# A streaming encoder step on one core: identity first, zero matmuls in a wait, constants moved up, and the last pair's first 256 tokens ahead

## The reference, cut to what matters

```python
h = rmsnorm(x, g_norm1)
qa, ka, va, qb, kb, vb, gates = split(h @ w_in)        # 1024 -> 4352
oa = sliding_window_attention(qa, ka, va, bias, sinks) # window 128, relative bias
ob = stick_breaking_attention(qb, kb, vb)
x = x + (sigmoid(g1) * (oa @ w_proj_a) + sigmoid(g2) * (ob @ w_proj_b)) @ w_out
u = square(relu(rmsnorm(x, g_norm2) @ w_up))           # 1024 -> 4096
x = x + u @ w_down                                     # 4096 -> 1024
y = rmsnorm(x, g_final)                                # returned, with new k and v rows
```

## Time and profile before

| | us |
|---|---|
| median of three runs (lowest, highest) | 858.58 (855.72, 858.74) |
| the profiled execution: its time | 855.1 |
| its span, first to last instruction | 853.2 |
| PE busy in it | 827.2 (97%) |
| DVE, ACT, POOL busy | 634.6, 385.3, 292.9 |
| share of the chain that ended last: PE, DVE, ACT, DMA | 84%, 11%, 2%, 1% |

### The profile page before, as it was taken

The page is one execution under the profiler, slowest core; times in us unless marked ns, Lnnn a source line. Parts: engine busy times, 40 slices in busy tenths (PEclk is TensorE's granted clock), DMA queues, the critical chain, the costliest instruction groups (busy, mean ns, idle before and its releaser), DMA issues.

```text
span 853.2 us, 16048 instructions
## 1 busy us (share of the span) xinstructions
PE 827.2 (97%) x6221; PEld 808.0 (95%) x6221; DVE 634.6 (74%) x1104; ACT 385.3 (45%) x642; POOL 292.9 (34%) x213
## 2 busy tenths in 40 slices
PE   8999999999999999999999999999999999999994
PEld 7899999999899999999999999999999999999994
DVE  4597887354698898968336889488975889488994
ACT  4646665233457686653433333333433343323431
POOL 2452222321644555334343400552025400552330
PEclk9999999999999999999999999999999999999997
DMA  8643111541111112232331313422133213412103
GB/s 268 236 159 97 52 51 33 179 161 50 51 50 50 49 50 68 80 112 101 122 99 53 96 51 99 127 73 80 54 112 108 89 49 98 140 57 94 55 1 112
DMA packets 68449, 78.18 MB, mean 92 GB/s; under 512 B 2552, under 2 KB 65072, under 8 KB 68016
## 3 DMA queue, kind: packets, MB, share of 16 engines
q1 hardware_dynamic: 67936, 76.39, 28.1%
q10 hardware_dynamic: 464, 1.12, 0.4%
HBM read 70.15 MB, written 8.93 MB: 93 GB/s over the span
## 4 chain that ended last, share of the span: by engine, by line
PE 84%; DVE 11%; ACT 2%; issue 1%; DMA 1%; SPq 0%; ACTq 0%; DVEq 0%
PE pan L1477 53%; PE pan L1688 13%; PE att L1688 11%; PE att L1626 1%; DVE sp_lo L1135 1%; DVE sp L1129 1%; PE pan L1529 1%; DMA x_rows<-in_x_prompt 1%; PE att L1599 1%; DVE sp_hi L1133 1%; DVE sp L1124 1%; PE att L1616 1%; ACT junk L570 1%; PE att L1766 1%; DVE m_a L1163 0%
## 5 line engine op out<-in xcount | busy, mean ns | idle before, releaser
L463 POOL TENSOR_TENSOR w_lo<-raw,w_hi 128x512 fp32r<-128x512 f32 x160 | 220.0, 1399 | 441.6 <-ACT w_hi L801 181.5
L1477 PE MATMUL pan<-a_hi,w_hi 128*128 128x288 f32 x624 | 134.5, 297 | 0.0
L1477 PE MATMUL pan<-a_lo,w_hi 128*128 128x288 f32 x624 | 133.0, 295 | 0.0
L1477 PE MATMUL pan<-a_hi,w_lo 128*128 128x288 f32 x624 | 133.0, 295 | 0.0
L1477 PE MATMUL pan<-h_hi,w_hi 128*128 128x288 f32 x512 | 109.8, 296 | 0.0
L1477 PE MATMUL pan<-h_hi,w_lo 128*128 128x288 f32 x512 | 109.7, 295 | 0.0
L1477 PE MATMUL pan<-h_lo,w_hi 128*128 128x288 f32 x512 | 109.6, 295 | 0.0
L1477 PEld LDWEIGHTS pan<-a_hi,w_lo 128*128 128x128 f32 x624 | 100.1, 188 | 0.0
L1477 PEld LDWEIGHTS pan<-a_lo,w_hi 128*128 128x128 f32 x624 | 99.9, 188 | 0.0
L1477 PEld LDWEIGHTS pan<-a_hi,w_hi 128*128 128x128 f32 x624 | 99.5, 188 | 0.3
L1688 PE MATMUL pan<-F_hi,w_hi 128*128 128x288 f32 x320 | 95.1, 297 | 0.0
(11 more groups left out here) (269 smaller groups left out, 1787.3 us busy)
## 6 DMA issues: line engine op xcount, KB each, us to landing
raw<-in_w_in SPq DMA_DIRECT2D x34, 512.0 KB, 4.8
raw<-in_w_up SPq DMA_DIRECT2D x32, 512.0 KB, 4.5
raw<-in_w_down SPq DMA_DIRECT2D x32, 512.0 KB, 4.7
raw<-in_w_out SPq DMA_DIRECT2D x8, 512.0 KB, 4.6
x_spill<-xT SPq DMA_DIRECT2D x1, 2304.0 KB, 7.1
xT<-x_spill SPq DMA_DIRECT2D x1, 2304.0 KB, 11.0
x_rows<-in_x_prompt SPq DMA_DIRECT2D x4, 512.0 KB, 8.2
raw<-in_w_pa SPq DMA_DIRECT2D x4, 512.0 KB, 4.0
```

The source lines that it names most:

```text
L463: last = nc.gpsimd.tensor_tensor(w_lo[:, slot, k:k + 4, :], raw[:, rs, k:k + 4, j * P:(j + 1) * P], w_hi[:, slot, k:k + 4, :].bitcast(F32) ...
L1477: got = nc.tensor.matmul(out[:, h, 0:HALF], w, x[:, h * HALF:(h + 1) * HALF], start=first and n == 0, stop=last and n == 2)
```

## The change

Seven edits:

1. ACT issues the load of `ident` ahead of those of `grow`, and PE transposes the first tile of x before it waits for `grow`.
2. PE runs 12 more matmuls on zeros (`on_zeros(12)`) between the second and the third tile of x, ahead of the wait for x piece 1.
3. ACT squares the samples (`squares(0, TT)`) before it waits for `frow`, not behind it.
4. DVE makes the constants before it waits for the sums of squares, not between the first two `take_qkv`.
5. In the last pair the products stand in another order: those that finish tokens 0 to 255 (`EARLY`) in tiles 6 and 7 come first. After the fifth product those tokens' squares are taken, their rows transposed and their sums made, while PE goes on with products six and seven.
6. The last norm is made twice: `token_rms(3)` for t = 0 and 1, `token_rms(4)` for t = 2, 3 and 4. The last squares are not added on DVE but summed by PE (`partial_sums` from `sq2`) in PSUM.
7. Rows are scaled and stored in the order 1 and 0 (early), then 2, 3 and 4. ACT scales row 0 in two halves; SP stores rows 1, 0 and 2 and the samples, ACT row 3.

```diff
+            act.dma_start(ident[:], consts[:, 0:P]).then_inc(ident_in, 16)
             act.dma_start(grow[0:KT, :], g1.rearrange("(k p) -> k p", p=P)).then_inc(grow_in, 16)
             act.dma_start(grow[KT:2 * KT, :], g2.rearrange("(k p) -> k p", p=P)).then_inc(grow_in, 16)
-            act.dma_start(ident[:], consts[:, 0:P]).then_inc(ident_in, 16)
...
+            squares(0, TT)
             act.wait_ge(frow_out, 1)
...
-            for n, t in enumerate((TT, 0, 1, 2, 3)):
-                squares(n, t)
+            for t in range(TT):
+                squares(t + 1, t)
...
-            square(0, 6, slice(0, TOK), 7 * 15 + 6, 16)
-            square(1, 7, slice(0, TOK), 7 * 15 + 7, 17)
-            root(3)
+            square(0, 6, EARLY, 7 * 15 + 4, 16)
+            square(1, 7, EARLY, 7 * 15 + 5, 17)
+            square(1, 7, LATE, 7 * 15 + 6, None)
+            root(3, slice(0, 2))
...
             act.wait_ge(rtok_ready, 3)
-            for t in (1, 3):
-                nc.scalar.activation(x_out[:, t, :], x_out[:, t, :], ACT.Copy, scale=rtok[:, t:t + 1]).then_inc(y_ready_a, 1)
...
+            act.wait_ge(xo_ready, 10)
+            scale(0, slice(0, D // 2))
+            square(0, 6, LATE, 7 * 15 + 7, None)
+            scale(0, slice(D // 2, D)).then_inc(y_ready_a, 1)
+            root(4, slice(2, TT + 1))
+            act.wait_ge(rtok_ready, 4)
+            act.wait_ge(xo_ready, 12)
+            scale(3, slice(0, D)).then_inc(y_ready_a, 1)
...
+            constants()
             dve.wait_ge(ss_ready, TT + 1)
...
             take_qkv(0, KA, 0)
-            constants()
             take_qkv(1, VA, 1)
...
             pe.wait_ge(ident_in, 16)
+            pe.wait_ge(x_in[0], 16)
+            x_out_tile(0)
             pe.wait_ge(grow_in, 2 * 16)
             nc.tensor.transpose(pan[:, 1, 1, 0:2 * KT], grow[:], ident[0:2 * KT, 0:2 * KT]).then_inc(gcol_out, 1)
-            pe.wait_ge(x_in[0], 16)
-            x_out_tile(0)
...
             x_out_tile(1)
+            on_zeros(12)
             pe.wait_ge(x_in[1], 16)
...
+            last_taken(3)
+            last_low(s_lo, 3)
+            product(last_a, 1, 0, 5, fresh=False).then_inc(prod_out, 1)
+            product(last_c, 3, 0, 3, (0, 2))
+            last_taken(5)
+            pe.wait_ge(xo_ready, 9)
+            last_rows(0, att[:, 3, :]).then_inc(xo_out, 1)
+            product(last_c, 3, 0, 3, (2, 4)).then_inc(prod_out, 1)
             pe.wait_ge(sq_added, 19)
-            feature_sums(2)
+            partial_sums(sq_sum, (0, 1), 0, start=True, stop=True).then_inc(ss_out, 1)
+            partial_sums(sq_sum, (2, 3, 4), 1, start=True)
+            last_taken(6)
+            last_low(s_lo, 2)
+            product(last_c, 0, 1, 2, fresh=False).then_inc(prod_out, 1)
+            pe.wait_ge(sq_ready, KT + 9)
+            partial_sums(sq2[:, 1, :], (2, 3, 4), 1)
+            last_rows(1, att[:, 2, :], tiles=(1,))
+            last_taken(7)
+            last_rows(1, att[:, 2, :], tiles=(0,)).then_inc(xo_out, 1)
```

More of the change, by code:

```diff
@@ L1455, in _ @@
             down_pair(3, 0)
-            for p in range(1, 4):
+            for p in range(1, 3):
                 down_pair(3, p, rows_1=lambda: take_rows(p - 1, 0), rows_2=lambda: take_rows(p - 1, 1), samples=lambda: take_samples(p - 1),
                           adds=lambda: add_pair(p - 1))
[L1459 to L1465, removed]
@@ L1466, in _ @@
-            for t in (0, 2, 4):
+            last_a, last_c = pan[:, 1, 0, 0:HALF], pan[:, 1, 1, 0:HALF]
+            take(3, 3, 1, 6, low, last_a)
+            low_4(3, 3)
+            low_3(3, 3)
+            take(3, 3, 2, 7, low, att[:, 0, 0:HALF], op=ALU.subtract)
+            take_rows(2, 0)
+            take(3, 3, 3, 6, high, last_a)
+            add_squares(4, 0)
+            take(3, 3, 4, 6, low, att[:, 1, 0:HALF], earlier=1)
+            take_rows(2, 1)
+            take_samples(2)
+            add_squares(5, 1)
@@ new lines, in _, with take_last_rows @@
+            dve.wait_ge(prod_out, 3 * 28 + 7 * 3 + 5)
+            dve.wait_ge(taken, 3 * 28 + (TAKEN0 + 7 * 3 + 2))
+            nc.vector.tensor_tensor(halves(xT[:, 7, :]), halves(xT[:, 7, :]), last_a.unsqueeze(1).to_broadcast([P, 2, HALF]), ALU.add).then_inc(taken, 1)
+            add_squares(6, 0, EARLY)
+            add_squares(7, 1, EARLY)
+            take(3, 3, 6, 7, high, last_c, earlier=5)
+            def take_last_rows(half, bank):
+                dve.wait_ge(xo_out, 10 + half)
+                rows = slice(2 * half, 2 * half + 2)
+                nc.vector.tensor_tensor(x_out[:, rows, 6 * P:D], bank.rearrange("p (t f) -> p t f", t=2),
+                                        gf_b[:, 6 * P:D].unsqueeze(1).to_broadcast([P, 2, 2 * P]), ALU.mult).then_inc(xo_ready, 1)
@@ L1471, in _ @@
+            token_rms(4, spread=False, cols=slice(2, TT + 1))
+            dve.wait_ge(xo_ready, 12)
+            for t in (2, 4):
+                scale_rows(t)
         @block.tensor
@@ L1509, in _, with on_zeros @@
             pe.wait_ge(warm_ready, 1)
-            for _ in range(24):
-                nc.tensor.matmul(pan[:, 0, 0, 0:2 * P], mask2[:, 0:P], mask2[:], start=True, stop=True)
+            def on_zeros(n):
+                for _ in range(n):
+                    nc.tensor.matmul(pan[:, 0, 0, 0:2 * P], mask2[:, 0:P], mask2[:], start=True, stop=True)
+            on_zeros(24)
             def x_out_tile(k):
@@ new lines, in last_rows, with partial_sums @@
+            def last_rows(half, bank, tiles=(0, 1)):
+                for t in range(2):
+                    for b in tiles:
+                        got = nc.tensor.transpose(bank[:, (2 * t + b) * P:(2 * t + b + 1) * P], xT[:, 6 + b, (2 * half + t) * P:(2 * half + t + 1) * P], ident[:])
+                return got
+            def partial_sums(src, ts, bank, start=False, stop=False):
+                for n, t in enumerate(ts):
+                    w = width(t)
+                    got = acc(att[0:w, bank, t:t + 1], src[:, t * P:t * P + w], ones1[:], start=start and n == 0, stop=stop)
+                return got
```

73 lines of the change are left out of this document (56 added, 17 removed).

## The result

Seven runs of each kernel: median 855.16 us (853.51 to 855.92) against 858.74 us (855.72 to 863.45), ratio 0.9945, 95% interval 0.9926 to 0.9964. The ratio makes the gain 0.55%, or 4.7 us of 858.7 (3.1 to 6.4); the medians lie 3.6 us apart and the means 4.3. The forecast was 5.1, and a median of 853.5. One execution in this document is left out of its ratio, one of e8 that took 1678 us, about twice the others.

The account below looks back on a forecast made before the run. PE, busy 97% of the span, was taken as the bound, so only the two ends could give much: start 1.9 plus end 3.2 makes 5.1 us, taking the median from 858.58 to 853.5 us; 8-in-10 range 850 to 857.

Parts of the forecast that it names:

- Rival A: Start gives little (0.5 us), as the clock falls and panel 4 takes up most; end 3.2; 854.9 us; chance 0.25.
- Rival B: End swallows its gain through slower hand-overs on DVE in the last pair; end gives 1.0; 855.7 us; chance 0.15.
- Identity first: Start: identity lands 1.0 us sooner, but tile 2 still waits for x piece 1, so value 0.
- Twelve zeros: Start: zero matmuls fill PE's wait for x piece 1 and may keep the clock; 0.4 us, at most 0.8.
- Squares: Start: samples' squares ahead of `frow` make the norm ready 1.2 us sooner; the spread moves by 0.9.
- Constants: Start: PE's 1.22 us wait for the second take goes; panel 4 waits for the third take, so 0.6 is kept.
- I carry the 1.9 through: Middle, from there to 826 us: no fixed times, so the start's 1.9 us gain was kept whole.
- Rival D: Slower: the clock falls elsewhere, 1.7 us of matmuls per fall; with six more falls 863.7 us; chance 0.04.
- Rival C: More: clock kept, no fall near 203 us, stores at their best; 7.5 us gained, 851.1 us; chance 0.14.
- The end: Last pair to span end: reordered products, split norm and early stores give 3.2 us, range 1.0 to 4.0.
- The issue term: End: fewer rows left to scale, so the last stores are issued at 845.0 and 845.3; gives 1.4 us.
- the stores' term: End: two stores leave early, the last 1.25 MB need 3.1 us plus 0.6 to 1.4; the rest of 3.2 us.

Follow-up runs that it names:

- e8: Changed kernel with DVE's three products with a gate behind its `sp_lo` instead of ahead; ratio to the kernel before 0.9976.
- e12: Changed kernel with e11's edit, and the order of DVE's first `a_lo` and of ACT's rounding changed; ratio to the kernel before 0.9914, median 853.28 us.
- e9: Changed kernel with the load of `ident` behind those of `grow` again (edit 1 undone, zeros kept); ratio to the kernel before 0.9942.
- e2: The kernel before with edits 5 to 7 (the end) alone; ratio to the kernel before 0.9970.
- e4: Changed kernel without the 12 matmuls on zeros (edit 2 undone); ratio to the kernel before 0.9958.
- e3: The changed kernel run again with no edit, for a second trace; ratio to the kernel before 0.9938, span 852.9 us.
- e6: Changed kernel with the samples' squares behind `frow` again (edit 3 undone); ratio to the kernel before 0.9967.
- e5: Changed kernel with the constants back between DVE's first two takes (edit 4 undone); ratio to the kernel before 0.9933.
- e11: Changed kernel with DVE's third take ahead of the second half of its `ka_lo` work; ratio to the kernel before 0.9941.
- e7: Changed kernel with three dense matmuls at three places in each of the two `sample_scores`; ratio to the kernel before 0.9988.
- e10: Changed kernel with SP's two early stores held back until row 2 is scaled; ratio to the kernel before 0.9986.
- e1: The kernel before with edits 1 to 4 (the start) alone; ratio to the kernel before 0.9981.

## Why the prediction was right, and where it was not

**The total** is right in size, 4.7 (3.1 to 6.4) against 5.1 us, by a sum whose terms were each somewhat off: the start gave 2.8 for 1.9, the end 2.45 for 3.2, and in the single trace the middle took both back. The measured median, 855.16, lies 1.7 above the forecast's 853.5 and nearer to the numbers of rivals A (854.9) and B (855.7). So the number alone doesn't choose between them; the traces do.

**Identity first, "Value 0"**: failed. I looked at who waits for the identity, and not at what its load does to those of x: with `ident` ahead of `grow` the pieces behind land some 0.5 us sooner. In ten traces with the zeros (all but e12, which has another order there) the product of tile 3 starts 6.0 us after piece 1's landing, whatever else was edited, so what the landing gains reaches the path: 0.5 us here, and 1.1 in e9, whose landing was late. Why the landing moves is open.

**Twelve zeros, 0.4 of at most 0.8**: too small, but the bound held. Counted from the landing of piece 1, the product of tile 3 starts at 6.0 us with them and at 6.8 and 6.7 without (before, e2): 0.7 to 0.8. My bound took the landing of the second weights at 13.2 us as fixed; it moved to 12.6 together with piece 1. Taken back alone (e4) they cost 1.5, since there piece 1 also landed 0.3 later than in e3 and the clock fell sooner. Identity and zeros together gave 1.3 to 1.4 where I had 0.4; this is most of the start's surplus.

**Squares, 0.9**: right. The spread moved by 2.2, which is this 1.3 to 1.4 and 0.8 to 0.9 more; e6 has 1.2, with 0.3 of it the landing. **Constants, 0.6**: 0.6 between the two traces (the spread moved 2.2, panel 4 2.8), 0.3 by e5. The step was right: the third take moved with the spread (44.46 to 42.16, 2.3), the transposes by 3.7, and 0.78 us of it ended as the wait on that take. e11 shows that nothing else stood behind it.

Taken back one at a time, the four cost 1.1, 1.5, 1.3 and 0.2 at the first scores, which is 4.2, while together they gave 2.8. Most of the surplus is not the edits': 0.5, 0.3 and 0.3 are the later landings of piece 1 in the traces of e9, e4 and e6. What is left is some 0.4 of overlap. `spread_rms` needs both PE's half panel and the norm, and the change made them ready within 0.4 us of each other (e3: `rrep` at 29.83, PE free at 30.20), so taking back either one's gain shows in full.

**"I carry the 1.9 through"** is the step that the profiled execution contradicts: the 2.8 us gained at 60 us were not there at 790, which was one of my own signs of a wrong forecast. The runs bear the step out on the mean. The time lost to half clock, estimated as in e7, was 10.0 us on the mean of 31 runs of the kernel before, 6.9 in 8 of the changed one (e3). Part of it is the stores' tail, where nothing is on PE: half clock lasts 8.6 and 8.0 us there in the two traces with the old end, and 5.9 on the mean of eleven with the new one (3.9 to 7.1, without e10), so 4.2 and 3.0 of these. So some 5.8 us were lost on the path before and 3.9 after, a difference of about one fall, which is the one at 11.8 us. Other falls of 3.4 or 6.8 us came at 172 to 182, 200 to 210, 315 to 322 or 353 to 360 us, one to three in a trace, whatever was edited. The profiled execution of before had one, and DVE's `sp_lo` were short at both places in it alone; its 855.1 us lie under all 88 timed runs of that kernel. It was a lucky execution and a poor stand-in for the median, and I had written only that two more falls would fit the spread.

**Rival D** (more falls by the change) is out: fewer, on the mean. The same program (kernel after and e3) fell at other places in two executions. The rule of the Trainium skill named in the prediction ("TensorE: Matmul & The Clock Gate", section "What's actually happening"), a window that runs freely, would have it so; the two traces agree. **Rival A** is out at the start; its wait on the third take was real. **Rival B** (hand-overs) had a grain: 1/rms of the late tokens came at 846.9 - 2.65 = 844.25, not 843.8. PE makes the late sums and transposes one after the other, and DVE's multiply of the samples' rows (845.81), which waits for the last of them, stands ahead of the Newton step. **Rival C** had the start nearest (0.8 + 1.5 = 2.3 of the 2.8); its second gain, no fall near 203 us, is seen in e1's trace alone, and the end gave less than its 3.5.

**The end, 3.2**: 2.45, by both terms. Product seven's issue ended at 840.7 (forecast 840.5), row 3 was issued at 845.5 (845.0), the samples, now last, at 845.7 (845.3); the wait within product six was 0.19 us (0.4). The issue term, last issue to last issue, was 1.0 of 1.4; the stores' term was 1.5 of 1.8, since the last 1.25 MB took 5.2 us from their first issue to the last landing, and I had 3.7 to 4.5 (which gives 849.1 to 849.9 from my 845.4, not 849.3 to 850.0). That early stores work e10 shows: 2.3 us, of which 1.1 are the issues. One sign contradicts the prediction's own sum: it has rows 1 and 0 leave at 841.8 and 842.3 and yet ahead of the take of product seven, which it has at 840.7. Measured, they left at 842.1 and 842.6, and the take began at 841.0.

## What to carry to other kernels

- Where two things meet (here PE's panel and the norm), ask of each edit what the other still needs; experiments that take one edit back can overstate its share. Before you compare two traces, look whether something else differs ahead of the edit: here the landing of one load, by 0.3 to 0.5 us.
- A small load put first or last in its queue is not free or worthless: look when the large loads of the other queue land (here 0.5 us sooner).
- A gain of 3 us at the start is real on the mean even if one trace has lost it by 350 us; compare the traces place by place, and use the granted clock of all runs to say how much of a difference is the clock's.

## What the runs showed that I had not expected

- The clock fell where PE was never idle: within or right behind 4.4 us of 64x64 matmuls (175 and 200 us), and nine dense matmuls among them did not stop it in the trace of e7.
- In the eight output panels (400 to 445 us) the cadence of a 288-column matmul at full clock was 130.0 ns in the kernel before, e1 and e2, and 133.3 in all that hold both halves of the change (after, e3 to e12), 1.2 us in all. It goes with the program and not with the time at which the stretch starts; the cause is open.
- The three `sp_lo` took 2.85 us for 1.76 at 351 us in every trace but that of before (and e8, which has another order), and at 313 us in all of these but the kernel after and e2. e2 is the same program as before up to there, and e3 the same as the kernel after, so it comes and goes by execution. Where they were short, POOL's product beside them took 2.1 us for 1.5.
